# Four modulation chunks in a row per quarter, and eight later ones inside the key projection: one core of a Trainium2, float32

## What is computed

```python
mod_x = silu(c) @ w_mod + b_mod            # 6 rows of 1024: sh1 sc1 gt1 sh2 sc2 gt2
mod_c = silu(c_ctx) @ w_mod + b_mod        # only sh1 and sc1 of it are used
h_x = rmsnorm(x, g_pre_mix) * (1 + sc1) + sh1
h_c = rmsnorm(ctx, g_pre_mix) * (1 + csc1) + csh1
u_x, q_x, k_x, v_x = split(h_x @ w_in)     # 512 columns each
k_c, v_c = ...(h_c @ w_in)
attn = neighbourhood_attention(q_x, k_x, v_x, k_c, v_c, rpb)   # 8 heads of 64
mix = concat(pool_mixer(u_x), attn) @ w_out
x = x + gt1 * rmsnorm(mix, g_post_mix)
y = square(relu((rmsnorm(x, g_pre_mlp) * (1 + sc2) + sh2) @ w_mlp_in)) @ w_mlp_out
x = x + gt2 * rmsnorm(y, g_post_mlp)
```

## Time and profile before

| what | value |
|---|---|
| median of 3 runs | 940.91 us (938.21 to 942.31) |
| profiled execution | 935.56 us, its span 933.7 us |
| PE busy | 869.5 us, 93% of the span |
| DVE busy | 522.0 us, 56% |
| ACT busy | 444.9 us, 48% |
| DMA moved | 165.87 MB, mean 178 GB/s |

### The profile page before, as it was taken

One profiled execution on the slowest core, in us unless ns is written; L12 is line 12 of the kernel. 1 busy time (PEld: TensorE's weight loads), 2 busy tenths in 40 slices (PEclk: granted clock), 3 DMA queues, 4 the chain that ended last, 5 costly groups with the idle time before them and its releaser, 6 DMA issues.

```text
span 933.7 us, 13970 instructions
## 1 busy us (share of the span) xinstructions
PE 869.5 (93%) x5434; PEld 738.1 (79%) x5434; DVE 522.0 (56%) x904; ACT 444.9 (48%) x797; POOL 44.6 (5%) x55
## 2 busy tenths in 40 slices
PE   4889989979999999899999999898888899999996
PEld 2588845758999998779999999786566699999995
DVE  2246066467776556565555554677455565555554
ACT  3274144255654444555444443665445554444442
POOL 1010000000000000000000000046100000000000
PEclk8789989999999999999999999998779999999999
DMA  9837069534786654437555555574012265555521
GB/s 347 325 138 292 0 228 343 191 120 146 260 289 231 194 188 158 136 136 246 180 183 184 198 179 168 178 239 159 0 46 68 91 194 189 184 191 178 192 91 46
DMA packets 45105, 165.87 MB, mean 178 GB/s; under 512 B 4976, under 2 KB 5104, under 8 KB 44784
## 3 DMA queue, kind: packets, MB, share of 16 engines
q1 hardware_dynamic: 45040, 164.98, 51.9%
HBM read 163.91 MB, written 1.05 MB: 177 GB/s over the span
## 4 chain that ended last, share of the span: by engine, by line
PE 86%; DVE 4%; ACT 3%; DMA 3%; issue 2%; POOL 1%; SPq 0%; ACTq 0%; DVEq 0%; POOLq 0%
PE ps L1359 13%; PE ps L1361 13%; PE ps L1360 13%; PE ps L1379 12%; PE ps L1381 12%; PE ps L1383 12%; DMA raw<-in_w_mod_p 3%; PE ps L1401 2%; PE ps L1600 2%; PE ps L1550 1%; PE ps L1787 1%; PE ps L1793 1%; ACT hi L450 1%; PE ps L1584 1%; ACT PT L462 1%
## 5 line engine op out<-in xcount | busy, mean ns | idle before, releaser
L866 DVE TENSOR_TENSOR lo<-raw,hi 128x1024 fp32r<-128x1024 f32 (+1 forms) x247 | 299.0, 1219 | 167.2 <-ACT hi L450 166.9
L1359 PE MATMUL ps<-Th,hi 128*128 128x256 f32 (+1 forms) x960 | 278.8, 290 | 10.5 <-DVE Tl L911 9.0
L450 ACT ACTIVATE hi<-raw 128x1024 fp32r<-128x1024 f32 (+1 forms) x247 | 257.1, 1049 | 60.4 <-PE ps L1383 59.9
L1361 PE MATMUL ps<-Th,lo 128*128 128x256 f32 (+1 forms) x960 | 277.4, 289 | 0.0
L1360 PE MATMUL ps<-Tl,hi 128*128 128x256 f32 (+1 forms) x960 | 277.3, 289 | 0.0
L1359 PEld LDWEIGHTS ps<-Th,hi 128*128 128x128 f32 x960 | 186.0, 194 | 19.8 <-issue 14.4
L1360 PEld LDWEIGHTS ps<-Tl,hi 128*128 128x128 f32 x960 | 186.2, 194 | 3.7
L1361 PEld LDWEIGHTS ps<-Th,lo 128*128 128x128 f32 x960 | 186.2, 194 | 1.3
L1379 PE MATMUL ps<-hi,Th 128*128 128x512 f32 (+2 forms) x524 | 178.3, 399 | 6.6 <-DVE lo L866 5.1
L1381 PE MATMUL ps<-lo,Th 128*128 128x512 f32 (+2 forms) x524 | 174.1, 391 | 0.0
L1383 PE MATMUL ps<-hi,Tl 128*128 128x512 f32 (+2 forms) x524 | 173.7, 390 | 0.0
(11 more groups left out here) (188 smaller groups left out, 625.9 us busy)
## 6 DMA issues: line engine op xcount, KB each, us to landing
raw<-in_ffn_down SPq DMA_DIRECT2D x44, 512.0 KB, 4.0
raw<-in_w_mod_p SPq DMA_DIRECT2D x40, 512.0 KB, 6.3
raw<-in_ffn_gate SPq DMA_DIRECT2D x40, 512.0 KB, 3.4
raw<-in_ffn_up SPq DMA_DIRECT2D x40, 512.0 KB, 3.3
raw<-in_w_mlp_out SPq DMA_DIRECT2D x32, 512.0 KB, 4.6
raw<-in_w_mlp_in SPq DMA_DIRECT2D x28, 512.0 KB, 4.5
raw<-in_w_out SPq DMA_DIRECT2D x16, 512.0 KB, 5.9
raw<-in_w_in_q SPq DMA_DIRECT2D x8, 512.0 KB, 3.5
```

Of the source, the lines that this page charges most:

```text
L450: e.activation(hi[h % RING][:, 0:w], raw[n % RAW][:, 0:w], ACT.Copy).then_inc(s_hi, 1)
L866: e.tensor_tensor(lo[h % RING][:, 0:w], raw[n % RAW][:, 0:w], hi[h % RING][:, 0:w], ALU.subtract).then_inc(s_lo, 1)
L1359: e.matmul(o, a, Th[:, k, c0:c1], start=(k == 0), stop=False)
L1361: return e.matmul(o, b, Th[:, k, c0:c1], start=False, stop=(k == KT - 1))
```

## The change

It has two parts. In the start, PE does the four products of quarter j in a row, then the transposes, then the u blocks of chunk 0, then turns the quarter, and only behind that come the u blocks of the other chunks. In the second part the chunks 16 to 23 leave near attention: chunks 16 and 17 come behind k chunk 1, 18 to 20 behind k chunk 2, 21 to 23 behind k chunk 3, in the stream's order as in PE's. Their products go to the banks ps2 and ps3, which the v projection needs too. So v chunk 0 is done in two halves: banks ps0 and ps1, then a wait until ACT and DVE have copied ps2 and ps3 out (`mod_part(0)`), then banks ps2 and ps3. `mod_turned(0)` stands ahead of v chunk 1. In near attention each step has two products, 16 in all. The v chunks stand behind chunk 23 in the stream, and chunks 24 to 29 right behind the v chunks.

```diff
@@ stream_plan
-    s += q + k + v + c[16:24]
+    s += q + k[0:2] + c[16:18] + k[2:3] + c[18:21] + k[3:4] + c[21:24] + v + c[24:30]
     for j in range(4):
-        s += o[j:j + 1] + c[24 + 4 * j:28 + 4 * j]
+        s += o[j:j + 1] + c[30 + 3 * j:33 + 3 * j]
@@ ACT
-                e.activation(acc[:, 0:512], ps[0][:, :], ACT.Copy).then_inc(s_rowA, 1)
+                e.activation(acc[:, 0:512], ps[0 if v else 2][:, :], ACT.Copy).then_inc(s_rowA, 1)
                 split(min(h + RING, CH["w_in_v", 3]))
+            mod_part(0)
             load_table(ACT.Exp)
-                    if n in (2, 5, 7):
-                        mod_part((2, 5, 7).index(n))
+                    if n in (3, 7):
+                        mod_part(n // 3)
@@ DVE
-                e.tensor_copy(acc[:, 512:1024], ps[1][:, :]).then_inc(s_rowD, 1)
+                e.tensor_copy(acc[:, 512:1024], ps[1 if v else 3][:, :]).then_inc(s_rowD, 1)
             for a in range(4):
                 window(a)
                 split(min(CH["w_in_k", a] + RING, CH["w_in_v", 3]))
+            mod_part(0)
@@ DVE, behind the four L957
+            e.wait_ge(s_rowT, 5)
+            e.tensor_tensor(sh2, ps[4][:, 0:8], col("b_sh2"), ALU.add).then_inc(s_mcol, 1)
@@ PE, the start
             for j in range(4):
-                mod_product(4 * j)
+                for n in range(4 * j, 4 * j + 4):
+                    mod_product(n)
+                turn_rows(0, j)
                 if j:
                     u_blocks(0, 2 * j - 2, 2 * j)
-                mod_product(4 * j + 1)
-                for g in range(1, j):
-                    u_blocks(g, 2 * j - 2, 2 * j)
-                if j == 0:
-                    turn_rows(0, 0)
-                if j == 1:
-                    turn_rows(0, 1)
-                mod_product(4 * j + 2)
-                if j >= 2:
-                    turn_rows(0, j)
-                    u_blocks(j, 0, 2 * j - 2)
-                mod_product(4 * j + 3)
-                if j:
-                    u_blocks(j, 2 * j - 2, 2 * j)
                 quarter_turned(j)
+                for g in range(1, j + 1):
+                    u_blocks(g, 2 * j - 2 if g < j else 0, 2 * j)
@@ PE, k and v
                 wstat(CH["w_in_k", a], ROT[a], 0, 512)
+                for n in range(*((16, 16), (16, 18), (18, 21), (21, 24))[a]):
+                    mod_product(n)
-                tstat(CH["w_in_v", j], [[0], [1], [2], [3]], lhs, 512, j == 0, j == 3).then_inc(s_used, 1)
+                if j == 0:
+                    for i in (0, 2):
+                        if i:
+                            e.wait_ge(s_rowA, 5)
+                            e.wait_ge(s_rowD, 1)
+                        mm = tstat(CH["w_in_v", j], [[i], [i + 1]], [row[i:i + 2] for row in lhs], 512, True, False)
+                    mm.then_inc(s_used, 1)
+                    continue
+                if j == 1:
+                    e.wait_ge(s_k, 2)
+                    e.wait_ge(s_const, 1)
+                    mod_turned(0, 4)
+                tstat(CH["w_in_v", j], [[0], [1], [2], [3]], lhs, 512, False, j == 3).then_inc(s_used, 1)
@@ PE, near attention
-                        for _ in range(MODS[n]):
-                            mod_product(at)
-                            at += 1
+                        mod_product(24 + 2 * n)
+                        mod_product(25 + 2 * n)
-                    if n in (4, 7):
-                        mod_turned(n // 7)
+                    if n == 5:
+                        mod_turned(1, 7)
```

More of the change, by code:

```diff
@@ L260, in build @@
         ATT = dict(n=32, tiles=(128, 256), heads=16, bufs=bufs2)
-        MODS = [3, 3, 2, 3, 3, 2, 4, 4]
         LAG = 4
@@ L985, in near_attention @@
                                         ALU.subtract).then_inc(s_nol, 1)
[L986 to L989, removed]
+                    if n == 6:
+                        e.wait_ge(s_rowT, 6)
+                        e.tensor_tensor(sc2, ps[7][:, 0:8], col("b_sc2"), ALU.add).then_inc(s_mcol, 1)
                     if n < 8:
@@ L1389, in mod_product @@
                 bank, c0 = (n // 4 % 2, n % 4 // 2 * L) if n < 16 else (quarter // 2, quarter % 2 * L)
+                if 16 <= n < 24:
+                    bank += 2
                 e.wait_ge(s_raw[at % RAW], lands(at))
@@ L1393, in mod_product @@
                 if n == 16:
+                    e.wait_ge(s_xTa, 16)
+                if n == 24:
                     e.wait_ge(s_vv, 4)
-                if n in (24, 32):
-                    e.wait_ge(s_rowA, n // 8 + 2)
-                    e.wait_ge(s_rowD, n // 8 - 2)
+                if n == 32:
+                    e.wait_ge(s_rowA, 6)
+                    e.wait_ge(s_rowD, 2)
                 for j in range(4):
@@ L1412, in quarter_turned, with mod_turned @@
                 m.then_inc(s_rowT, 1)
-            def mod_turned(v):
+            def mod_turned(v, bank):
                 e.wait_ge(s_rowA, v + 5)
@@ L1418, in mod_turned @@
                 for j in range(KT):
-                    at = 8 * v + j
-                    m = e.matmul(ps[7][:, at:at + 1], acc[:, j * P:(j + 1) * P], ones[:, 0:1], start=True, stop=True)
+                    m = e.matmul(ps[bank][:, j:j + 1], acc[:, j * P:(j + 1) * P], ones[:, 0:1], start=True, stop=True)
                 m.then_inc(s_rowT, 1)
@@ L1500, in near_attention @@
             def near_attention():
-                at = 16
+                e.wait_ge(s_mcol, 1)
                 for n in range(10):
```

## The result

The changed kernel took 928.18 us (median of 4 runs, 924.63 to 929.46), the kernel before 939.72 in the same count (938.21 to 942.31). The ratio is 0.9868, with a 95% interval of 0.9831 to 0.9906: faster by 1.3%, some 12 us, where 9.6 us were forecast. The profiled execution of the changed kernel took 929.46 us with a span of 927.5, against 935.56 and 933.7.

What follows compares the result with a forecast made beforehand. PE was taken as the path nearly everywhere, except in the start and near attention, where it waits. Terms -10.0 + 5.3 + 7.9 + 1.7 - 14.5 = -9.6 us gave 931.3 from the 940.91 median; range 923.5 to 938.5.

Steps and rivals of the forecast that it cites:

- The start: Up to q's first matmul: quarter turns come earlier, the last at 37 instead of 48.33; -10.0 us, between -7 and -12.
- The key projection: In k: eight products and the turn of the row move onto a part where PE is already the path; +5.3 us.
- The wait: Between v chunk 0's halves: PE waits for DVE's copy behind its windows; +7.9 us, between +6 and +11.
- The clock behind it: After the wait at v chunk 0: a stretch at half clock; +1.7 us, between 0 and +3.4.
- Near attention: Two products per step, no DMA waits, step set by DVE at 4.79 us; -14.5 us, ends -10 and -16.
- (1): Rival: the start stays with stream and clock, gaining 3 to 4 us; -3.3 in all, 937.6 us; chance 0.15.
- (2): Rival: no wait at v, DVE's copy coming in time; 9.6 us more gained, 921.7 us; chance 0.10.
- (3): Rival: a longer wait at v, 12 to 14 us; total -4, 937 us; chance 0.08.
- (4): Rival: near attention at half clock, 4.4 us more per step; with five steps +12.4, 953.3 us; chance 0.07.
- The sum: All terms to the end of near attention: -9.6 us, with nothing behind that point changed.

Runs made afterwards that it cites:

- start_only: Kernel before with only the new order of the start (four products in a row, u blocks behind the turn): 927.29 us, ratio 0.9863.
- copy_first: Changed kernel with DVE's copy that frees bank ps3 moved ahead of the pool windows: 919.62 us, ratio 0.9763 against the kernel before.
- later_only: Changed kernel with PE's old order of the start, keeping the changed stream order: 935.65 us, ratio 0.9998 against the kernel before.
- products_twice: Changed kernel with the first product of each near attention step done twice on PE, which alters part of the output: 926.73 us in a single run.
- after_again: Changed kernel run once more with no edit: 928.26 us, ratio 0.99 against the kernel before.
- blocks_ahead: Changed kernel with the blocks of u chunks 1 to 3 back ahead of a quarter's turn: 929.86 us, ratio 0.9917 against the kernel before.
- split_early: Changed kernel with the next u chunk's split done inside a quarter on ACT and DVE: 923.31 us, ratio 0.985 against the kernel before.
- o_later: Changed kernel with every `w_out` chunk of near attention one modulation chunk later in the stream: 930.61 us, ratio 0.9927 against the kernel before.
- best_o_later: Changed kernel, DVE's ps3 copy before the windows, ACT's ps2 copy after second k bank, u splits inside quarters, `w_out` chunks one modulation chunk later: 915.52 us.

## Why the prediction was right, step by step

- **The start, -10.0, measured -10.5.** The turns were forecast at 14.5, 22.2, 29.0 and 37 and came at 15.25, 21.93, 31.74 and 37.93. The third was late by 2.7 us: I took its chunks as landing by 26.3 as before. But chunk 9's buffer hangs on the `lo` of u chunk 1, which was made 1.45 us later (20.38 instead of 18.93), and its transfer then took 4.8 us instead of 3.7. It landed at 26.5 and the last of the quarter at 29.0. The gap closed again in the fourth. Over seven profiles the term is nearer to -8, and start_only's ratio puts it between 8 and 18 us: the step holds, and the agreement to 0.5 us is luck, since the single profile was one of the better ones. The chain of turns was right about the waits (some 5 us). That the clock would rise as well was in my sum only as "no gap that would bring its clock down" behind the last turn, and it gave some 3 us on average and about 6 in this profile.
- **The key projection, +5.3, measured about +6.3.** k took 26.25 us instead of 21.8, so 4.5 for eight products and not 3.5: each group of products between long matmuls costs some tenths more than in near attention. The turn was 1.8 without its share of the low clock. I also wrote that the stream rests in k. It does not: its DMA share there was 0.74, and it rested in v (0.01). This did no harm, as PE waited for no chunk in k.
- **The wait, +7.9, measured +7.0.** The chain through `lo` of v chunk 0, windows, splits and copy was forecast to end 35.9 us behind the start of k and ended at 36.1; PE came to the wait 29.3 us behind the start of k and not 28.0, mostly because of its products. copy_first shows the cause, and later_only has the same 7.0.
- **The clock behind it, +1.7, measured +2.8.** The whole second half of v chunk 0 ran at about half clock and part of the turn too, so the upper end was nearer.
- **Near attention, -14.5, measured -14.4.** The size was right by luck: what was off inside it cancelled. I said that DVE's 4.79 us set the step; products_twice shows that PE's 4.57 do. I said that no chunk would be late: chunk 35 was, by 1.29 us in this profile. And counted from the first scores, step 3 began at 10.5 us and not at 11.7, while the end came 7.8 us behind the start of step 7 and not 6, where I had kept 1.2 for a stretch at half clock that did not come. I took some 2 us for the clock behind step 7; over the whole stage it gave 6.4. The stage also varies: 38.3 to 41.5 us in the profiles with its new order and no product added, and 54.2 and 56.4 with the old one.
- **The rivals.** (1), a start held by stream and clock, happened in part: over the seven profiles k began up to 4.3 us later than in the earliest, with more of the start at the lower clock. (2) and (3) did not, the wait was 7.0. (4), near attention at half clock, did not: its mean PEclk was 1.00.
- **The sum.** -8.4 us at the end of near attention, against -9.6. The 2.2 us given back in the untouched rest go with the granted clock. That stretch took between 760.7 and 765.6 us in the thirteen profiles of this study, and its length follows its time at half clock: 38.6 us of it in the kernel before (763.2), 48.7 in the changed kernel (765.4), 38.6 again in after_again (763.3). Six more profiles have 48.7 us or more of it, and there the stretch took 765.4 to 765.6. Between the two profiles the kernel gained 6.2 us, between the medians 11.5; that the second lies nearer to the forecast is in part luck.

## What to carry to other kernels

When an engine's copy frees a buffer for a later stage, look at what stands ahead of that copy in its engine's order, and not only whether the engine is idle on average: here DVE sat idle for 12 us, then did 12 us of work that had been well hidden, and PE stood for 7 of them. Moving work to where a resource rests (chunks into the key projection, so that the stream could work on through v, where it had been idle: DMA share 0.36 instead of 0.01) pays only if the work's own hand-over, here two copies and a turn, doesn't become the new wait. And where an in-order engine waits for a slow chain, put first what starts that chain and what frees the stream's buffers, and behind it the work that needs neither.

## What was not expected of the hardware

One program's start of some 30 us differed by 2.6 us between two executions, with a mean granted clock of 0.94 in one and 0.84 in the other. The same start in seven kernels ended over a range of 4.3 us (k at 60.4 to 64.7), with PE's idle time the same within 0.9 us. In near attention the clock fell behind sixteen 128x1 matmuls in five profiles (blocks_ahead, split_early, after_again, o_later, best_o_later) and in six others with the turn at this place it did not. In the stretch of o_later shown above, PE was counted busy all the time. Between two executions of one program even a wait can change, as that for chunk 35 did (1.29 and 0.46 us). So a change of under 5 us in this kernel can't be told from four runs. A trace can show it where a wait far larger than such differences goes, as the 7.0 us did, but a small wait that is gone from a single trace proves nothing.
